# Latent attention: non-rotary score terms ahead of the rotary ones, the rotation one piece earlier, conditioning sums on other pieces

## The reference

```python
q = (rmsnorm(c_q, q_norm) @ w_uq).reshape(B, S, 8, 128 + 64)
q = concat([q[..., :128], rope(q[..., 128:], pos)])
kv = (rmsnorm(c_kv, kv_norm) @ w_ukv).reshape(B, S, 8, 128 + 128)
k = concat([kv[..., :128], broadcast(rope(k_rope, pos))])   # one rotary key for all heads
y_c = softmax(causal(q @ k.T / sqrt(192))) @ kv[..., 128:] * silu(mla_gate)
y_d = rmsnorm((softmax_1 - lam * softmax_2) @ v) * silu(diff_gate)
x = x + concat([y_c, y_d]) @ w_out
```

## Time and profile before

| what | value |
|---|---|
| runs (3) | 2862.36, 2867.10, 2867.46 us; median 2867.1 |
| profiled execution, its time | 2870.17 us |
| profiled execution, span | 2868.5 us |
| mean granted TensorE clock | 0.978 of full |
| busy share | PE 95%, DVE 61%, ACT 45% |
| chain that ended last | PE 82%, DVE 7%, ACT 3%, DVE queue 3%, DMA 2% |
| first `mla` unit, first matmul of piece 0 | 679.85 us from the span's start |

### The profile page before, as it was taken

One profiled execution on the slowest core, in us unless ns is written; L12 is line 12 of the kernel. 1 busy time (PEld: TensorE's weight loads), 2 busy tenths in 40 slices (PEclk: granted clock), 3 DMA queues, 4 the chain that ended last, 5 costly groups with the idle time before them and its releaser, 6 DMA issues.

```text
span 2868.5 us, 49783 instructions
## 1 busy us (share of the span) xinstructions
PE 2737.6 (95%) x19249; PEld 2568.2 (90%) x19249; DVE 1763.1 (61%) x2244; ACT 1280.6 (45%) x1670; POOL 18.4 (1%) x33
## 2 busy tenths in 40 slices
PE   7999999998889799999999999999999999999997
PEld 7998789998777699999999987879999999999786
DVE  6777878777656755555556535456675454555544
ACT  5556444554443434443343334444444444444443
POOL 1000000000000000000000000000000000000000
PEclk9999999998889899999999999999999999999999
DMA  6565866655537365555548644547685555555554
GB/s 185 151 196 159 271 185 204 186 178 173 162 129 271 104 197 167 176 177 185 174 156 277 207 147 154 188 144 250 228 292 180 186 182 181 181 180 185 175 189 139
DMA packets 450700, 534.50 MB, mean 186 GB/s; under 512 B 32955, under 2 KB 343750, under 8 KB 449670
## 3 DMA queue, kind: packets, MB, share of 16 engines
q1 hardware_dynamic: 447840, 522.29, 57.5%
q0 software_dynamic: 2064, 10.11, 1.1%
q10 hardware_dynamic: 662, 0.25, 0.0%
HBM read 530.46 MB, written 2.10 MB: 186 GB/s over the span
## 4 chain that ended last, share of the span: by engine, by line
PE 82%; DVE 7%; ACT 3%; DVEq 3%; DMA 2%; issue 2%; ACTq 0%; SPq 0%
PE banks L1742 16%; PE banks L1744 16%; PE banks L1743 16%; PE banks L1753 8%; PE banks L1754 8%; PE banks L1755 8%; DVE w_lo L1159 3%; ACT w_hi L656 2%; PE banks L1991 1%; PE banks L2120 1%; PE banks L2137 1%; PE banks L1899 1%; DVEq L1150 1%; DMA w_raw<-in_od_w_in 1%; DMA w_raw<-in_l_w_in 1%
## 5 line engine op out<-in xcount | busy, mean ns | idle before, releaser
L1159 DVE TENSOR_TENSOR w_lo<-w_raw,w_hi 128x1024 fp32r<-128x1024 f32 (+2 forms) x848 | 974.5, 1160 | 834.1 <-ACT w_hi L656 814.0
L656 ACT ACTIVATE w_hi<-w_raw 128x1024 fp32r<-128x1024 f32 (+2 forms) x848 | 844.4, 1005 | 1088.5 <-PE banks L1744 606.1
L1742 PE MATMUL banks<-act_hl,w_hi 128*128 128x256 f32 x4304 | 1249.1, 290 | 36.0 <-DVE w_lo L1159 17.1
L1744 PE MATMUL banks<-act_hl,w_lo 128*128 128x256 f32 x4304 | 1226.0, 285 | 0.0
L1743 PE MATMUL banks<-act_hl,w_hi 128*128 128x256 f32 x4304 | 1225.9, 285 | 0.0
L1742 PEld LDWEIGHTS banks<-act_hl,w_hi 128*128 128x128 f32 x4304 | 832.9, 194 | 52.3 <-DVE w_lo L1159 18.7
L1743 PEld LDWEIGHTS banks<-act_hl,w_hi 128*128 128x128 f32 x4304 | 832.9, 194 | 3.8 <-issue 2.4
L1744 PEld LDWEIGHTS banks<-act_hl,w_lo 128*128 128x128 f32 x4304 | 832.5, 193 | 0.0
L1753 PE MATMUL banks<-w_hi,act_hl 128*128 128x512 f32 (+3 forms) x1440 | 509.5, 354 | 26.4 <-DVE x_res L1505 7.5
L1754 PE MATMUL banks<-w_lo,act_hl 128*128 128x512 f32 (+3 forms) x1440 | 506.9, 352 | 0.0
L1755 PE MATMUL banks<-w_hi,act_hl 128*128 128x512 f32 (+3 forms) x1440 | 506.2, 352 | 0.0
(11 more groups left out here) (270 smaller groups left out, 1586.5 us busy)
## 6 DMA issues: line engine op xcount, KB each, us to landing
w_raw<-in_od_w_in SPq DMA_DIRECT2D x256, 512.0 KB, 4.5
w_raw<-in_ev_w_in SPq DMA_DIRECT2D x256, 256.0 KB, 3.6
w_raw<-in_l_w_in SPq DMA_DIRECT2D x96, 512.0 KB, 4.3
w_raw<-in_l_w_in SPq DMA_DIRECT2D x128, 256.0 KB, 3.2
ada_ring<-in_ada_w SPq DMA_DIRECT2D x128, 256.0 KB, 4.3
w_raw<-in_l_w_out SPq DMA_DIRECT2D x64, 512.0 KB, 4.9
y_mix<-in_ada_w SPq DMA_DIRECT2D x128, 256.0 KB, 3.1
const_b<-in_ada_w SPq DMA_DIRECT2D x128, 256.0 KB, 4.5
```

The source lines that it names most:

```text
L656: last = nc.scalar.activation(dst(w_hi[:, p % RING, :]), src(w_raw[:, p % RING, :]), ACT.Copy)
L1159: last = tt(dst(w_lo[:, p % RING, :]), src(w_raw[:, p % RING, :]), dst(w_hi[:, p % RING, :]).bitcast(F32), ALU.subtract)
L1742: mm(out, hi, a[:, kt, 0:T], start=start, stop=False, skip_group_check=True)
L1744: return mm(out, lo, a[:, kt, 0:T], start=False, stop=stop, skip_group_check=True)
```

## The change

It has four parts.

1. PE's scores of a latent unit: first the non-rotary products of both heads (4 matmuls), then a wait for `mla_rope`, then the rotary products of both heads (4 matmuls). Before, the wait stood ahead of all eight, and the two kinds took turns.
2. The rotation on DVE moves from hook 3 to hook 2, so ahead of the split of piece 3. PE's `rot64` product goes to bank 7 in place of bank 5, which now holds the early scores.
3. Conditioning steps: in each `diff` unit 10 steps, on pieces 0 to 4 and 9 to 13 (before 8, on the odd pieces); in `mla` none in unit 0 and 8 each in units 1 to 3, on pieces 4, 5, 5, 5, 6, 6, 6, 7 (before one on every piece of all four units). The number over all three stages stays 72. A group's sums in `mla` go ahead of piece 5 (before piece 3), its columns are read after piece 7 (before 6), and the first of the two groups moves from unit 1 to unit 0.
4. PE waits for `ada_cols_read` (`s_acol`) 7 before the last latent unit's `rot64` product, since both use bank 7.

```diff
-_units += [("cq", i, range(8)) for i in (1, 2)] + [("diff", i, range(1, 16, 2)) for i in range(4)]
-_units += [("mla", i, range(8)) for i in range(4)] + [("out1", 1, range(8))]
+_units += [("cq", i, range(8)) for i in (1, 2)] + [("diff", i, (0, 1, 2, 3, 4, 9, 10, 11, 12, 13)) for i in range(4)]
+_units += [("mla", i, (4, 5, 5, 5, 6, 6, 6, 7)) for i in (1, 2, 3)] + [("out1", 1, range(8))]
...
-                at = (7, 10, 13) if stage == "diff" else (7 if stage == "mla" else 2, 3, 6)
+                at = (7, 10, 13) if stage == "diff" else (7, 5, 7) if stage == "mla" else (2, 3, 6)
...
-                if p == 3:
+                if p == 2:
                     ve.wait_ge(s["rot"], i + 1)
-                    tt(mla_qr, PS[:, 5, 0:T], sin64, ALU.mult)
+                    tt(mla_qr, PS[:, 7, 0:T], sin64, ALU.mult)
                     tt(mla_qr0, mla_qr0, cos64, ALU.mult)
                     drain()
                     tt(mla_qr, mla_qr, mla_qr0, ALU.add).then_inc(s["rope"], 1)
+                if p == 3:
                     ve.wait_ge(s["scores"], i + 1)
                     scores_max(mla_s, range(2), causal, 5, s["max"])
...
-                    2: [step(mla, 3, n), *mixes("out1", 0, 1, 2), step(mla, 4, n)],
+                    2: [step(mla, 2, n), step(mla, 3, n), *mixes("out1", 0, 1, 2), step(mla, 4, n)],
...
-                    mm(half(5, 0), rot64, mla_qr0, start=True, stop=True, skip_group_check=True)\
+                    mm(half(7, 0), rot64, mla_qr0, start=True, stop=True, skip_group_check=True)\
...
+                    parts = ((0, 128, 0, P), (128, 384, P, T))
+                    for h in range(2):
+                        for lo, hi, q0, keys in parts:
+                            mm(PS[:, 5 + h, lo:hi], q[:, h, q0:q0 + P], k[:, h, 0:keys], start=lo == 0, stop=False,
+                               skip_group_check=True)
                     te.wait_ge(s["rope"], i + 1)
-                    pairs = [[(q[:, h, :], k[:, h, :]), ropes[h]] for h in range(2)]
-                    sets_scores(pairs, 5).then_inc(s["scores"], 1)
+                    for h, (rq, rk) in enumerate(ropes):
+                        for lo, hi, q0, keys in parts:
+                            r = mm(PS[:, 5 + h, lo:hi], rq[:, q0:q0 + P], rk[:, 0:keys], start=False, stop=True,
+                                   skip_group_check=True)
+                    r.then_inc(s["scores"], 1)
...
                 n = COUNT["mla"] - 1
+                te.wait_ge(s_acol, 7)
                 mla(0, n)
                 mla(1, n)
```

More of the change, by code:

```diff
@@ L75 @@
 _units = [("swa", i, (0, 1, 5, 6)) for i in range(4)] + [("out0", i, range(8)) for i in (1, 2, 3)]
-_units += [("cq", i, range(8)) for i in (1, 2)] + [("diff", i, range(1, 16, 2)) for i in range(4)]
-_units += [("mla", i, range(8)) for i in range(4)] + [("out1", 1, range(8))]
+_units += [("cq", i, range(8)) for i in (1, 2)] + [("diff", i, (0, 1, 2, 3, 4, 9, 10, 11, 12, 13)) for i in range(4)]
+_units += [("mla", i, (4, 5, 5, 5, 6, 6, 6, 7)) for i in (1, 2, 3)] + [("out1", 1, range(8))]
 ADA_AT, ADA_SUM = {}, {}
-for _s, _i, _ps in _units:
-    for _p in _ps:
-        ADA_AT[_s, _i, _p] = (len(ADA_AT),)
+_where = [(s, i, p) for s, i, ps in _units for p in ps]
+for _n, _at in enumerate(_where):
+    ADA_AT[_at] = ADA_AT.get(_at, ()) + (_n,)
 _first = [(s, i) for s in ("swa", "out0", "cq", "diff", "mla", "out1") for i in range(COUNT[s])]
 for _n in range(8):
-    _s, _i, _p = list(ADA_AT)[ADA_K * (_n + 1) - 1]
+    _s, _i, _p = _where[ADA_K * (_n + 1) - 1]
     ADA_SUM[_first[_first.index((_s, _i)) + 1]] = _n
```

## The result

| | before | after |
|---|---|---|
| median of the runs shown, us | 2867.28 (2862.36 to 2867.81) | 2829.86 (2827.64 to 2830.26) |
| profiled execution, us | 2870.17 | 2829.45 |
| its span, us | 2868.5 | 2827.8 |
| PE busy in the span, us | 2737.6 | 2710.5 |

The ratio is 0.987, 95% interval 0.9856 to 0.9884: 37.4 us faster. One execution of the changed kernel took 7413 us; it is left out of the range and the ratio but counted in the median, which is 2829.45 without it (37.8 us faster).

The account below looks back on a forecast made before the run. PE, busy 95% of the span, was taken as the bound. 24.2 + 6.0 + 4.5 + 3 + 2.8 - 7.6 = 32.9 us off 2870.2 gave 2837.3; the median runs 3.1 lower, so 2834 us, range 2823 to 2848.

Parts of the forecast that it names:

- `diff`: `diff` units 1 to 3: step on piece 7 gone from before the transposes, 4.5 us; clock staying up, 3 of 0 to 5.
- latent unit 0: Latent unit 0 loses all eight steps and takes one group's sums; two shorter waits gain 1.5 and 1.3, 2.8 us.
- last scores: Scores before `out1`: grouping gains, but three splits still precede the rotation, so 0.7 us of its wait is left.
- Scores: Four latent units: each set of eight products takes 2.3 us in place of 6.5; with the wait, 24.2 us gained.
- The wait on the rotation: PE's wait before latent scores, 8.1 us in four: goes in units 1 to 3, 0.7 left around `out1`.
- The slow stretch behind the scores: Matmuls at half clock behind the scores of latent units 1 to 3 go: 2.0 us a unit, 6.0 us gained.
- The back half: Latent units 1 to 3: eight steps behind the softmax make PE wait 1.8 and 1.3 us a unit, costing 7.6 us.
- rival B: Clock still falls at the latent scores because of new idle time: 12.9 us given back, 2847 us; 9%.
- The signs: Trace signs of being right, such as latent units 1 to 3 each 7 to 9 us shorter, scores about 2.3 us.
- A: Latent units 1 to 3: bursts of steps make loads come 4 us late, 12 us lost, 2846 us; 13%.
- D: Slower than before: steps beyond the four-slot ring wait for landings in latent units 1 to 3, 2874 us; 2%.
- C: Rotation no earlier, DVE waiting for `rot64`'s product with piece 3's split behind it; only grouping gained, 2857 us; 4%.

Follow-up runs that it names:

- experiment 3: Changed kernel with the two kinds of score products taking turns again behind the wait, rotation still in hook 2: 2840.18 us.
- experiment 4: Changed kernel with only the rotation put back in hook 3, behind the split of piece 3: 2829.59 us.
- experiment 1: Kernel before plus the changed scores and earlier rotation, conditioning steps left on their old pieces: 2836.35 us, ratio 0.9892.
- experiment 2: Changed kernel with only the new step table kept: score products take turns behind the wait, rotation back in hook 3, bank 7 stays: 2843.14 us.
- Experiment 5: Changed kernel with one step of each `diff` unit put back on piece 7 in place of piece 4: 2839.51 us.
- experiment 9: Changed kernel with the steps of latent units 1 to 3 on pieces 0, 2, 3, 4, 5, 6, 6, 7: 2822.89 us.
- experiment 6: Changed kernel with the steps of latent units 1 to 3 on pieces 0, 2, 4, 5, 6, 6, 7, 7: 2829.69 us.
- experiment 8: Changed kernel with latent steps on pieces 0, 2, 4, 5, 6, 6, 7, 7 and `out1`'s first three mixes made early: 2824.27 us.

## Why the prediction came out as it did

The forecast was 2834 us in a range of 2823 to 2848. Measured 2829.86: inside, and 37.4 us where 32.9 were summed. Set beside its terms, with 1.8 us of sums counted in unit 1 where the forecast had them:

| part | forecast, us | measured, us |
|---|---|---|
| `diff` | 4.5 + 3 | 9.8 |
| latent unit 0 | 2.8 | 4.2 |
| units 1 and 2, each 2.0 + 4.2 + 2.0 - 3.1 | 5.1, 5.1 | 5.8, 5.1 |
| unit 3, 2.0 + 4.2 + 2.0 - 1.4 | 6.8 | 7.0 |
| last scores, 2.0 + 4.2 - 0.7 | 5.5 | 5.9 |

**Scores: right in mechanism and size.** Forecast 2.3 us a set; measured 2.3, the four non-rotary pairs 1.4 of it (746.88 to 748.28, forecast 1.3) and the rotary ones 0.9 (forecast 1.0). The rule that the prediction weighed, from the Trainium skill (TensorE: Matmul & The Clock Gate, Part 3, The mechanism), a weight load overlaps only when its row group differs, isn't borne out for these products: by it the four non-rotary pairs would have taken 0.17 us more each, 2.0 in all. (The same section of the Trainium skill also lets a load go ahead into a background weight buffer, so its rule is less strict than the prediction put it.) The 0.17 came from a row of products in turns, and it is there that the time goes: 0.63 us for 256 columns in experiment 3, where the grouped non-rotary products, 1.4 us for two of 128 and two of 256 columns, leave some 0.47 by columns.

**The wait on the rotation: gone, and in more places than forecast.** The last unit's 0.7 isn't there either: with the new table the wait ahead of products in turns is 1.71 us (experiment 3), and in the changed kernel 1.5 us of non-rotary products and 0.26 of waiting for ACT's copy (L662) stand ahead of it, so the rotation, done at 808.46, is in time for 808.67. But the reason was put half wrong. The forecast let the moved rotation and the moved steps act together; experiment 4 shows that the move of the rotation adds nothing, and experiment 1 that with both in front of the non-rotary products even the old steps leave no wait. In units 1 to 3 any two of the three (steps away, rotation earlier, rotary products last) remove it; experiment 2, with the steps away alone, keeps 0.72 in units 2 and 3. The earlier rotation alone and the later rotary products alone were not run. Before `out1`, where no steps moved, only rotary products behind the others do (experiments 2 and 3 keep 1.71).

**The slow stretch behind the scores: right.** The forecast was 2.0 us a unit. Experiment 1 measures wait, scores and stretch together, with the old table and so without the costs of the back half: the units are 8.8, 8.7 and 8.1 us shorter than before and the last scores 5.7, against 8.2 each and 5.5. Experiments 2 and 3 say why: turns without a wait, or behind 0.72 us, stay at full clock, and turns behind a wait of 1.7 us do not. What made the stretch slow was the wait ahead of these products, and in experiment 2 the fall began inside it; the turns alone only made the scores longer.

**`diff`: the term that was mis-sized.** The wait went from 2.86 to 1.36 as forecast, 4.5 us in three units. For the clock I took 3 us of 0 to 5, and 9.8 - 4.5 = 5.3 came, 5.7 if counted from the first late split. It held in all three units, 1.00 behind each of the transposes. Experiment 5, which brings wait and slow clock back together, bears the mechanism out. The Trainium skill (TensorE: Matmul & The Clock Gate, Part 4: PE-mode transpose) says that transposes do not count as busy for the clock. The fall that the prediction drew from it did not come: after 1.36 us of idling and 0.7 of transposes the clock was 1.00. This doesn't test the rule, since 2.92 us of plain idling had left the clock at full too. I had a row on either side and took the middle, and nothing in the rows said how often each would happen.

**Unit 0: 1.4 us too low.** The waits went from 6.54 to 4.74 and from 2.92 to 1.55, 3.2 us together against 2.8. The rest fits the clock, whose low stretch behind the first wait is shorter now; the forecast had no term for it.

**The back half: 7.6 forecast, 7.8 measured** (experiments 1 and 9), but made up otherwise. The stalls were 1.35 and 1.06 in unit 1, 1.86 in unit 2, and 0.89 in unit 3, 5.2 us in place of 7.6; the slow stretch behind the 1.86 us adds most of the rest. That the two sums agree is in part luck. That a new stall could bring its own slow clock was in rival B alone.

**The signs.** The prediction also wrote down, as a sign of being right, that each of the units 1 to 3 would be shorter by 7 to 9 us. They were shorter by 7.6, 5.1 and 7.0, so unit 2 misses. That line did not fit the prediction's own sum, whose terms give 5.1 for unit 2 (and 6.9 for unit 1 with its sums gone); 7 to 9 is what they give without the new waits of 3.1 us.

**Rivals.** A and D, loads that come late: they do come late, and it costs nothing. ACT waits for piece 7 of unit 3:

```profile
797.59 1.26 ACT L656 ACTIVATE w_hi<-w_raw 128x768 fp32r<-128x768 f32 x2 [5.06 <-DMA w_raw<-in_l_w_uq]
```

but DVE is busy without a gap from 789.85 to 801.6 with the steps and the piece-6 split, so PE's 0.89 us at 801.71 is DVE's own queue. In units 1 and 2 the copy of piece 7 is likewise ready before DVE comes to its split (733.8 against 734.87, 765.9 against 767.7). B, the clock falls at the scores: it doesn't, and it does once behind a stall, the smaller form. C: PE never waits for the split of piece 3.

## What to carry to other kernels

When two kinds of accumulating products share a wait that only one of them needs, put the kind that needs nothing first and the wait between them: here it hid the wait, kept the granted clock at full, and saved the dearer starts of products that take turns, 1.8 us for eight even at full clock. Steps of background work that are moved out of a critical path have to be placed by the next split that stands behind them on their engine, over the edge of a unit too: the same eight steps cost 7.8 us packed, nothing gained when two stood on the last piece, and nothing lost at all with one there. And one short step in front of a wait of the bounding engine can cost more than its length, since the clock can fall with the idle time: one step of 1.5 us in each unit of `diff` cost 9.7 us in all, 8.4 of them in three units.

## What was not expected of the hardware

Products that take turns between 128 and 64 rows take longer from start to start than the same ones in groups, with no idle time between them and at granted clock 1.00: eight in 4.1 against 2.3 us. Whether the clock falls behind an idle time of PE could not be told here from the time's length. It stayed at full behind all idle times of 0.72 to 1.56 us in `diff` and units 1 to 3, and fell behind those of 1.63 and 2.16 in the kernel before, 1.73 and 2.09 in experiment 6, 1.86 in the changed kernel and 2.87 in experiment 5. But it held behind the 2.92 before unit 1, in the kernel before and in experiment 1, and behind these two, of 1.83 us in experiment 2 and of 2.09 in experiment 8:

```profile
769.21 0.39 PE L1742 MATMUL banks<-c_norm,w_hi 128*128 128x256 f32 x1 [1.83 <-DVE w_lo L1159]
```

```profile
769.00:773.00 4.00, 3.79 (x32) 3.79 (x33) 3.82 (x7) 1.26 (x2) 0.00 (x0) 1.00 0.98 330
```

```profile
771.68 0.39 PE L1749 MATMUL banks<-act_hl,w_hi 128*128 128x256 f32 x1 [2.09 <-DVE w_lo L1165]
```

```profile
772.00:776.00 4.00, 4.00 (x34) 3.94 (x33) 3.49 (x6) 3.06 (x5) 0.00 (x0) 1.00 0.71 220
```

The last is the same wait at the same place of the same table of steps as in experiment 6, where the clock fell. So a slow stretch seen in one trace, such as the one behind the 1.86 us, is not certain in every execution, and no run here settles what else decides.
